# The last of six modulation parts: from matrix products on the TensorE to running sums on the VectorE

## The reference

```
mod = silu(cond) @ w_mod + b_mod          # two rows: the request's, the context's
sh1, sc1, gt1, sh2, sc2, gt2 = six parts of mod, 2048 columns each
h = rmsnorm(x, g1) * (1 + sc1) + sh1
... gated linear attention (branch A), windowed attention (branch B) on h @ w_in
merged = sigmoid(gate_a) * (o_gla @ w_branch_a) + sigmoid(gate_b) * (o_swa @ w_branch_b)
x = x + gt1 * (merged @ w_out)
h2 = rmsnorm(x, g2) * (1 + sc2) + sh2
aff = softmax(h2 @ w_router); each of 16 experts takes its top tokens (64 latent + 16 context = 80)
x = x + gt2 * sum over experts of gate * (silu(xs @ Wg) * (xs @ Wu)) @ Wd
y = rmsnorm(x, g_final)
```

## Time and profile before

| | us |
|---|---|
| median of 3 runs | 2985.25 (2982.33 to 2985.82) |
| the profiled execution, its own time | 2982.53 |
| its span in the trace | 2980.7 |
| PE busy | 2837.4 (95%) |
| DVE busy | 2062.2 (69%) |
| ACT busy | 1607.4 (54%) |
| POOL busy | 281.0 (9%) |

### The profile page before, as it was taken

The page is one execution under the profiler, slowest core; times in us unless marked ns, Lnnn a source line. Parts: engine busy times, 40 slices in busy tenths (PEclk is TensorE's granted clock), DMA queues, the critical chain, the costliest instruction groups (busy, mean ns, idle before and its releaser), DMA issues.

```text
span 2980.7 us, 38357 instructions
## 1 busy us (share of the span) xinstructions
PE 2837.4 (95%) x13981; PEld 2100.4 (70%) x13981; DVE 2062.2 (69%) x2384; ACT 1607.4 (54%) x1943; POOL 281.0 (9%) x182
## 2 busy tenths in 40 slices
PE   6899899999999999999999987999999999999993
PEld 4798548899668888888888873666666666666662
DVE  2436655544866766677655556888888888888884
ACT  4345324444854444444343434777777777777773
POOL 0000010000000000000010000111221122111111
PEclk9999999999999999999999998999999999999996
DMA  9822342221023333433362279999999999999994
GB/s 373 291 71 71 123 167 85 76 75 57 1 73 128 132 140 113 157 128 113 137 259 71 84 287 364 401 403 400 383 382 381 389 388 386 378 387 389 388 393 163
DMA packets 160779, 684.72 MB, mean 230 GB/s; under 512 B 13940, under 2 KB 14020, under 8 KB 99004
## 3 DMA queue, kind: packets, MB, share of 16 engines
q1 hardware_dynamic: 147216, 613.45, 53.4%
q0 software_dynamic: 11408, 69.78, 7.4%
q10 hardware_dynamic: 2064, 0.26, 0.1%
HBM read 651.91 MB, written 31.60 MB: 229 GB/s over the span
## 4 chain that ended last, share of the span: by engine, by line
PE 91%; DVE 4%; ACT 2%; DMA 1%; issue 1%; POOL 0%; DVEq 0%; POOLq 0%; ACTq 0%; SPq 0%
PE ps L855 38%; PE ps L1319 24%; PE ps L1346 12%; PE ps L874 5%; PE ps L881 3%; PE ps L1292 1%; PE ps L1146 1%; PE ps L1157 1%; PE ps L819 1%; PE ps L1024 1%; PE ps L1128 1%; PE ps L1256 1%; PE ps L989 1%; DVE ar L1835 0%; PE ps L801 0%
## 5 line engine op out<-in xcount | busy, mean ns | idle before, releaser
L855 PE MATMUL ps<-split_weights,split_tokens 128*128 128x512 f32 x5040 | 1159.0, 391 | 4.4 <-issue 2.9
L855 PEld LDWEIGHTS ps<-split_weights,split_tokens 128*128 128x128 f32 x5040 | 945.2, 188 | 212.8 <-issue 11.5
L1319 PE MATMUL ps<-split_experts,split_xsT 128*80 128x512 f32 x3072 | 709.3, 392 | 4.9 <-DVE split_experts L2074 4.9
L480 DVE TENSOR_TENSOR split_weights<-ring,split_weights 128x512 fp32r<-128x512 f32 x384 | 266.4, 694 | 540.7 <-ACT split_tokens L477 538.6
L476 ACT ACTIVATE split_weights<-ring 128x512 fp32r<-128x512 f32 x384 | 242.7, 632 | 736.8 <-PE ps L855 611.7
L1319 PEld LDWEIGHTS ps<-split_experts,split_xsT 128*80 128x80 f32 x3072 | 454.9, 148 | 257.4 <-DVE split_experts L2074 5.8
L2074 DVE TENSOR_TENSOR split_experts<-hT,split_experts 128x2048 fp32r<-128x2048 f32 x240 | 548.0, 2289 | 75.6 <-ACT split_experts L1657 75.4
L1657 ACT ACTIVATE split_experts<-hT 128x2048 fp32r<-128x2048 f32 x240 | 460.7, 1920 | 153.2 <-PE ps L1319 111.8
L1346 PE MATMUL ps<-split_experts,split_hidT 128*80 128x512 f32 x1536 | 361.0, 394 | 0.0
L1346 PEld LDWEIGHTS ps<-split_experts,split_hidT 128*80 128x80 f32 x1536 | 225.5, 148 | 121.9
L483 DVE TENSOR_TENSOR split_tokens<-hT,split_tokens 128x640 fp32r<-128x640 f32 x304 | 250.5, 824 | 0.0
(11 more groups left out here) (261 smaller groups left out, 1929.0 us busy)
## 6 DMA issues: line engine op xcount, KB each, us to landing
ring<-w_mod SPq DMA_DIRECT2D x96, 1024.0 KB, 5.3
hT<-w_exp_gate SPq DMA_DIRECT2D x80, 1024.0 KB, 7.2
hT<-w_exp_up SPq DMA_DIRECT2D x80, 1024.0 KB, 7.1
hT<-w_exp_down SPq DMA_DIRECT2D x80, 1024.0 KB, 9.5
ring<-w_in SPq DMA_DIRECT2D x64, 1024.0 KB, 5.2
ring<-w_exp_gate SPq DMA_DIRECT2D x32, 1024.0 KB, 8.0
ring<-w_exp_up SPq DMA_DIRECT2D x32, 1024.0 KB, 10.3
ring<-w_exp_down SPq DMA_DIRECT2D x32, 1024.0 KB, 7.6
```

Source lines behind the costliest of these rows:

```text
L480: a = self.eng.tensor_tensor(spW[:, s, 1, :], raw, spW[:, s, 0, :].bitcast(F32), ALU.subtract)
L855: mm = pe.matmul(ps[:, b, :], spX[:, s, x, b * P:(b + 1) * P], spW[:, s, w, :], start=(k == 0 and x == w), stop=(k == n_k - 1 and x == 1))
L1319: mm = pe.matmul(ps[0:CAP, bank + i, :], xsT[:, x, k, :], spE[:, s, w, col:col + BANK], start=(k == 0 and x == w), stop=(k == KT - 1 and x ...
```

## The change

- `G_GATE` now has 24 granules a stripe instead of 20: each of the 12 gate granules is followed by one of w_mod, and granules 8 to 11 of these are of part 5. Every gate piece, those next to the ends of products included, has one row of modulation behind it.
- There are six accumulators instead of four, and three sums by TensorE per stripe: the first 512 columns of the stripe's sh2/sc2 (`part` 0) after piece 20, the second 512 (`part` 1) after piece 37, and 512 columns of gt2 (`part` 2) after piece 6 of the next stripe, or after piece 7 of the out stage for the last stripe. 12 sums in all. ScalarE's copies and GpSimd's additions to DRAM go with them.
- The granules `G_M4`, all `mod_granules` of part 5 and ScalarE's copy L1393 for it are gone. The router's weights are loaded by GpSimd in the out stage.
- Expert 0: seven granules instead of five are loaded ahead of the choice of tokens (the first two into ring slots, as soon as the out stage has left them). ScalarE splits the first three during the choice of tokens, VectorE right after it, and the split of the gathered tokens comes behind these on both engines.

The core of the diff (declarations, numbers of semaphores and the SyncE order of loads shortened):

```diff
-G_OUT = G_GATE + 4 * 20
-G_M4 = G_OUT + 4 * 4
+G_OUT = G_GATE + 4 * 24
+MOD_ROWS = [[k] for k in range(48)]
...
             def mod_sums(k):
-                j, kk = (first + k) // 4, (first + k) % 4
-                if j % 3 == 2:
-                    return
+                dve = sp.eng
+                for r in MOD_ROWS[first + k]:
+                    m, kk = r // 4, r % 4
+                    part, row, g = m // 4, r % KT, G_GATE + mod_place(m)
...
-                        if first + k in (22, 46):
-                            mod_sum(n, (first + k) // 24, before)
+                        if first + k == 6 and before is not None:
+                            mod_sum(before, 2)
+                        if first + k == 20:
+                            mod_sum(n, 0, None if before is None else n * NT + (NT - 1 - NT))
+                        if first + k == 37:
+                            mod_sum(n, 1)
...
             def with_merged(k):
                 if 1 <= k <= NT:
-                    merged_transpose(3, k - 1)
+                    merged_transpose(3, k - 1, 12)
+                if k == NT + 2:
+                    mod_sum(3, 2, 4 * NT - 1)
...
             pe.wait_ge(sq_part, NT)
-            mod_granules(3)
...
             mm.then_inc(af_tr, 1)
-            mod_granules(7)
             pe.wait_ge(tk_d, 1)
...
-            mod_granules(3)
             pe.wait_ge(xs_ld, 16)
             pe.wait_ge(af_cp, 1)
             xs_transposes(0, 12, xs_first)
             xs_transposes(12, KT, xs_tr)
-            mod_granules(3)
-            pe.wait_ge(mc_ev, 10)
...
 ScalarE:
+            act.wait_ge(x1_st, 16 * NT)
+            for i, n in enumerate((2, 2, 1)):
+                act.wait_ge(n2_st[i], 16 * n)
+            split_expert(0, 0, AHEAD)
             act.wait_ge(xs_tr, 1)
             copy_xs(0, 2)
             copy_xs(2, 3)
-            mod_part(1)
-            split_expert(0, 0, AHEAD)
 VectorE:
+            low_expert(0, 0, AHEAD)
             dve.wait_ge(xs_h, 2)
             low_xs(0, 3).then_inc(xs_l, 1)
-            low_expert(0, 0, AHEAD)
```

More of the change, by code:

```diff
@@ L283, in build @@
         mrow = area(27216, NT, BANK)
-        mtmp = [area(13056 + BANK * b, BANK) for b in range(4)] + [area(29776, BANK)]
+        mtmp = [area(12800 + BANK * b, BANK) for b in range(5)]
         x1 = area(0, NT, D)
@@ L291, in build @@
         arows = cst[:, P:P + D]
-        mod_acc = cst[:, P:P + 4 * BANK].rearrange("p (j w n) -> p j w n", j=2, w=2)
-        mod_ones = cst[:, P + 4 * BANK:P + 4 * BANK + 32]
+        mod_acc = [cst[:, P + BANK * i:P + BANK * (i + 1)] for i in range(5)] + [area(29776, BANK)]
+        mod_ones = cst[:, P + 5 * BANK:P + 5 * BANK + 32]
+        g2_half = area(12800, BANK)
         gt2 = area(28240, D)
@@ L396, in gate_split @@
-            sp.pieces(P_GATE + first, n * 48, lambda k: G_GATE + gate_place((first + k) // 4), n * 5,
+                dve = sp.eng
+                for r in MOD_ROWS[first + k]:
+                    m, kk = r // 4, r % 4
+                    part, row, g = m // 4, r % KT, G_GATE + mod_place(m)
+                    v = ring[:, g % SLOTS, kk * BANK:(kk + 1) * BANK]
+                    if kk == 0:
+                        dve.wait_ge(slot_ready[g % SLOTS], n * 96 + 16 * (g // SLOTS + 1))
+                    if row == 0:
+                        dve.wait_ge(s_mT, n * 3 + (part + 6))
+                    for who in range(2):
+                        acc, c = mod_acc[2 * part + who], cond32[:, row, who:who + 1]
+                        if row == 0:
+                            dve.tensor_scalar(acc, v, c, None, ALU.mult).then_inc(z_rd, 1)
+                        else:
+                            dve.wait_ge(z_rd, n * 96 + (2 * GH + 32 * part + 2 * row + who))
+                            dve.scalar_tensor_tensor(acc, v, c, acc, ALU.mult, ALU.add).then_inc(z_rd, 1)
+                    if kk == 3:
+                        dve.wait_ge(z_rd, n * 96 + (2 * GH + 32 * part + 2 * row + 3))
+                        dve.sem_inc(slot_used, 1)
@@ L397, in gate_split @@
+            sp.pieces(P_GATE + first, n * 48, lambda k: G_GATE + gate_place((first + k) // 4), n * 6,
                       (hT, oT, hT, swT)[q], lo, hi, mod_sums)
@@ L653, in _ @@
                 pool.dma_start(final, st[:, s % 2, 9, :]).then_inc(st_out, 16)
-            mod_part(2, 1)
+            pool.wait_ge(mc_ev, 1)
+            for g in range(4):
+                col = 2 * D + g * BANK
+                pool.dma_start(mod_dram[:, col:col + BANK], modc[32 * g:32 * g + 2, :],
+                               accum_op=ALU.add).then_inc(mc_st, 16)
             pool.wait_ge(st_out, 16 * 2 * GH)
@@ L1189, in merged_transpose, with mod_sum @@
                 mm.then_inc(mt_pe, 1)
[L1191 to L1197, removed]
+            def mod_sum(n, part, bank_copied=None):
+                pe.wait_ge(z_rd, n * 96 + (2 * GH + 1 + 32 * (part + 1)))
+                if bank_copied is not None:
+                    pe.wait_ge(mt_cp, bank_copied)
+                pe.wait_ge(mc_ev, n * 3 + (1 + part))
                 for who in range(2):
-                    mm = pe.matmul(ps[32 * who:32 * who + 32, 7, :], mod_ones, mod_acc[:, half, who, :],
+                    mm = pe.matmul(ps[32 * who:32 * who + 32, 7, :], mod_ones, mod_acc[2 * part + who],
                                    start=True, stop=True)
```

124 lines of the change are left out of this document (51 added, 73 removed).

## The result

| | before | after |
|---|---|---|
| median of 5 runs, us | 2985.52 (2982.33 to 2989.77) | 3005.28 (3002.88 to 3005.83) |
| the profiled execution, its own time | 2982.53 | 3005.83 |
| its span | 2980.7 | 3004.0 |

The change makes the kernel slower: ratio 1.0066, interval 1.0054 to 1.0078, 19.8 us at the medians. The forecast had the direction and, with +13.3 us (2997, range 2988 to 3002), too little.

What follows compares the result with a forecast made beforehand. TensorE, holding 91% of the chain, was taken as the bound. +13.4 (sums) + 0 + 0 - 0.1 (start of expert 0) = +13.3 us gave 2995.8 or 2998.5, stated as 2997, range 2988 to 3002.

Steps and rivals of the forecast that it cites:

- Part 1, the sums: Gate stage: 12 sums at new places paid in full, 1.22 us each, less one paid before; +13.4 us.
- -1.3: End of stripe 3: the one old sum paid in full, 1.28 us, goes away.
- the shadow: Branch ends: seven old sums cost nothing, since TensorE waits there for VectorE's products anyway.
- only the new sums are paid: Rival, gate stage: eight old sums merely moved, four new ones cost +4.9 us; 2987 to 2990, chance 0.14.
- cost nothing: Rival: sums cost nothing anywhere, the start of expert 0 decides; 2977 to 2980, chance 0.06.
- Part 2, the rows on VectorE: Gate stage: 64 more pieces get a 1.41 us row on VectorE, hidden under TensorE's 3.40 us; cost 0.
- The rival of VectorE as the bound: Rival, branch ends: rows not worked off before the products, 5.6 us at seven ends, up to 3035; chance 0.04.
- Part 3: Part 5's products leave TensorE; h2 transposes still start at the lower clock; 0, at worst 1.5 us more.
- Part 4, the start of expert 0: From indices to expert 0's first matmul: -5.4 + 4.0 + 1.3 = -0.1 us, ends -5.4 and +3.
- What goes: Expert 0: from the transposes' end to the first matmul 3.1 us instead of 8.51; -5.4.
- +1.90 + 0.55 + 1.59 = +4.0: Expert 0: GpSimd's index copy, gap and gather instruction lengthen beside VectorE's weight splits; bounds 0 and +7.
- I keep 4.93: Expert 0: the gather's landing stays 4.93 us after its instruction, despite three or four expert loads beside it.

Runs made afterwards that it cites:

- e4: Changed kernel with the sums of the first two parts back behind pieces 22 and 46, the third left behind piece 6; 2993.16 us, ratio 1.0039.
- e6: Changed kernel with the two matmuls of each of its 12 sums done twice; 3014.97 us, ratio 1.0102.
- e1: Changed kernel, VectorE's splits of expert 0's weights wait for a count behind GpSimd's gather instruction; 2997.79 us, ratio 1.0044.
- e2: Changed kernel, SyncE issues expert 0's eighth and later weight granules only after the gathered tokens have landed; 2999.96 us, ratio 1.0054.
- e11: e5 with idle matmuls on TensorE, 4 ahead of the gathered tokens' transposes and 3 behind them; 2981.48 us, ratio 0.9991.
- e8: e3, but VectorE's splits wait for a small GpSimd copy behind the gather's instruction instead of a count; 2992.32 us, ratio 1.0026.
- e3: Changed kernel with the edits of both e1 and e2; 2993.37 us, ratio 1.0032.
- e5: Changed kernel with the edits of e4 and e8 together; 2982.90 us, ratio 0.9994 against the kernel before.
- e10: e5 run once more, unchanged; 2982.87 us, ratio 0.9990 against the kernel before.

## Why the prediction was wrong

- **Part 1, the sums: right in its mechanism, 0.7 us too small.** +13.4 forecast for the gate stage; the trace has +14.10 to the first h2 transpose. The price of a sum holds: stripes 0 to 2 have eight sums and take 9.7 us more (855.81 to 1371.74, before 852.40 to 1358.59), 1.22 each. One term was too large: the paid sum of before at the end of stripe 3, "-1.3", gave back 0.83 only (from ScalarE's start at the release of piece 46 to the first transposes of the out stage 11.22 us before, 10.39 now); why is open. Another 0.3 lies between the out stage's second stripe and h2, where VectorE now waits for the rows loaded into hT. e4 confirms the shadow at seven ends, e6 that a sum elsewhere is paid in full. The rivals "only the new sums are paid" and "cost nothing" fall with e4 and e6; the former is what e4 itself reaches, once the sums stand where the shadow is.
- **Part 2, the rows on VectorE: right.** Cost 0. No piece in mid-product has TensorE waiting for VectorE, and e4 leaves 4.93 us for four sums of 1.22. The rival of VectorE as the bound falls.
- **Part 3: right,** the h2 transposes start at the same lower clock and take 3.65 (3.64 before).
- **Part 4, the start of expert 0: the step that failed.** What goes was right: from the transposes' end to the first matmul 3.2 us (forecast 3.1). What comes had two mis-sized terms. *The gather held up, "+1.90 + 0.55 + 1.59 = +4.0"*, measured +6.4: I took the row of the steady run because "the instructions beside are the same, back to back in both". They are not. In the kernel before, an operation of 0.48 us that reads PSUM stands behind the subtraction that the copy meets (copy 1883.49 to 1885.57):

```profile
1883.24 2.29 DVE L2074 TENSOR_TENSOR split_experts<-hT,split_experts 128x2048 fp32r<-128x2048 f32 x1 [0.22 <-ACT split_experts L1657]
...
1885.44 0.48 DVE L2055 TENSOR_TENSOR split_xsT<-ps,split_xsT 128x320 fp32r<-128x320 f32 x1
```

  Here three subtractions follow one another, and GpSimd's copy got in behind none of them. My upper end had this case, the value hadn't. e1 shows that the subtractions are the cause. *The landing, "I keep 4.93"*, measured 9.02: I saw that three or four loads would take the place of two, and still took the row of before as the near end; I bounded it below and not above. The trace of the kernel before had a bound. Its first gather took 5.86 us from the issue to the landing; for all 18, most of them beside a stream of expert loads (and with an instruction 1.6 us longer), it gives

```profile
DMA to landing us min/median/max: 5.7/10.2/11.8
```

  and in the changed kernel the first one takes 9.95. In the kernel before the two loads came behind the gather's instruction; now four come ahead of it, the first by 6.5 us, three of them let out by VectorE's early subtractions. e2 shows it: 4.49 without them. Against these, *the transposes, "+1.3"*, measured +0.1 (2.41 after 2.33): I took 2.33 as their price with TensorE at work, but its granted clock was 1.00 only up to 1822.0 and 0.54 in the rest of them, so there was little left to lose; at 1.00 throughout they took 2.15 (e11). The 3.64 of transposes of 128x128 didn't carry over to these of 80x128.
  The first expert, counted at nothing, is 0.7 us longer (71.18 to 70.44), at the lower clock for about 5 us instead of about 3.4.
- In sum part 4 is -0.1 forecast and +5.8 measured: -5.3 + 6.4 + 4.1 + 0.1 + 0.7, and 0.2 less between h2 and the indices. This is what carried the time past the range; of its terms the landing was enough by itself (3005.3 less 4.1 is 3001.2, inside), and the copy without it was not (with -2.4 the time is 3002.9). The rule of the Trainium skill ("GPSIMD Engine Reference", Specifications, on the shared SBUF interfaces) pointed at the right place, and the trace agrees: 6.58 us beside three subtractions, 0.18 without. That section gives no size.

## What to carry to other kernels

Ask of an idle time at an edge which wait it belongs to: work put there is free (seven sums here), and moving it to a seemingly calm stretch costs it in full. Before work is brought forward into an engine's gap, see what GpSimd has to issue at that moment, and which loads the work will let go; a short wait for each of the two was worth about 11 us here.

## What the runs showed of the hardware

- A GpSimd copy of 0.18 us took 2.08 beside one 128x2048 fp32 subtraction of VectorE that was followed by an operation with a PSUM input, and 6.58 beside three in a row: it ended with the last one (1838.82 and 1838.78).
- A semaphore that GpSimd counts up behind an indirect DMA fires before the instruction has run (VectorE started at 1830.99, the instruction at 1831.18). A small GpSimd copy behind it, with the count on it, does order them (e8: the instruction takes 0.98 us instead of 2.95).
- A gather of 80 rows of 8 KB landed 4.3 to 4.7 us after its instruction with no weight load beside it (e2, e3, e5, e8, e10, e11), 4.9 with two loads of 1 MB issued behind it (before), and 7.6 to 9.6 with three or four issued ahead of or beside it (after, e1, e4, e6).
- With idle matmuls TensorE's granted clock rose from 0.50 to 1.00 between 1822 and 1824 us in e11 and stayed there over the 3 us in which the tokens were split, which three more of them filled (TensorE busy 2.54 of the 3.00 us from 1828 to 1831). In e5, without them, it was 0.50 until 1838.
